# Two transformer blocks on one core: the order at the norms, at the start, in the logits, and the mixing of two attention maps

## The reference

```python
for i in range(4):                                   # first block
    q, k, v, ..., qm = split_cols(x @ w_in_...)
    mix = dsa_attention / dilated_attention / moba_attention(q, k, v, ...)
    mo  = memory_attention(qm, *split(layer_norm(mem) @ w_mem_kv[i]))
    x = layer_norm(ALPHA * x + concat(mix, mo) @ w_out[i], ln1_g[i], ln1_b[i])
    x = layer_norm(ALPHA * x + (silu(g) * u) @ w_down[i], ln2_g[i], ln2_b[i])   # g, u = x @ w_gate_up[i]
for l in range(2):                                   # second block
    h = rms_norm(x, norm_pre[l]);  u = h @ w_in[l]
    # differential attention: two softmax maps of each of four heads
    s  = einsum('bqhmd,bkhmd->bhmqk', q, k) * scale + bias
    pm = softmax(s)
    oa = einsum('bhqk,bkhe->bqhe', pm[:, :, 0] - lam * pm[:, :, 1], v)
    oa = rms_norm(oa, da_subln[l]) * (1 - lam_init)
    ...                                              # latent and sliding-window attention, three gated branches
    x = x + rms_norm(y @ w_out[l], norm_post[l])
    x = x + sigmoid(x @ w_ple_gate[l]) * (p[l] @ w_ple_proj[l])
```

## Time and profile before

| what | value |
|---|---|
| median of 3 runs | 1969.3 us (1964.08 to 1973.55) |
| profiled execution, its own time | 1971.21 us |
| its span, first to last instruction | 1969.2 us |
| mean granted clock of PE | 0.988 |
| PE busy | 1892.0 us, 9682 matmul records |
| DVE, ACT, POOL busy | 817.6, 938.9, 1520.2 us |

### The profile page before, as it was taken

The page is one execution under the profiler, slowest core; times in us unless marked ns, Lnnn a source line. Parts: engine busy times, 40 slices in busy tenths (PEclk is TensorE's granted clock), DMA queues, the critical chain, the costliest instruction groups (busy, mean ns, idle before and its releaser), DMA issues.

```text
span 1969.2 us, 27526 instructions
## 1 busy us (share of the span) xinstructions
PE 1892.0 (96%) x9682; PEld 1551.4 (79%) x9682; DVE 817.6 (42%) x1921; ACT 938.9 (48%) x1473; POOL 1520.2 (77%) x1332
## 2 busy tenths in 40 slices
PE   7999999999999999999999999989899999989998
PEld 6777888777888887788887688877888877878876
DVE  7774111356211345411067621035736344545634
ACT  4454444354444346444335644444447644545752
POOL 7767979885797987697977778795677886777784
PEclk9999999999999999999999999999999999999999
DMA  8444656564666564466545456654544555554452
GB/s 280 121 145 148 194 152 233 172 183 134 181 191 211 156 192 150 147 185 198 189 144 162 159 154 178 211 184 117 165 149 146 172 170 179 156 169 137 136 172 93
DMA packets 184269, 330.54 MB, mean 168 GB/s; under 512 B 12188, under 2 KB 44488, under 8 KB 184136
## 3 DMA queue, kind: packets, MB, share of 16 engines
q1 hardware_dynamic: 176224, 323.21, 53.1%
q10 hardware_dynamic: 7912, 5.59, 1.0%
HBM read 325.35 MB, written 3.41 MB: 167 GB/s over the span
## 4 chain that ended last, share of the span: by engine, by line
PE 79%; DVE 8%; POOL 7%; DMA 3%; issue 2%; ACT 1%; ACTq 0%; DVEq 0%
PE acc L1376 22%; PE acc L1378 22%; PE acc L1377 21%; POOL w_lo L1160 7%; PE tps L1327 4%; PE acc L1391 3%; PE tps L1409 2%; PE ops L1433 2%; DMA raw<-in_w_down 1%; DVE U L1798 1%; DVE small L1485 1%; PE acc L1351 1%; PE acc L1352 1%; PE acc L1353 1%; PE ops L1339 1%
## 5 line engine op out<-in xcount | busy, mean ns | idle before, releaser
L1160 POOL TENSOR_TENSOR w_lo<-raw,w_hi 128x512 fp32r<-128x512 f32 (+2 forms) x1244 | 1479.5, 1226 | 411.5 <-ACT w_hi L1188 410.2
L1188 ACT CAST w_hi<-raw 128x1024 fp32r<-128x1024 f32 (+2 forms) x624 | 615.8, 991 | 765.7 <-PE acc L1378 641.1
L1376 PE MATMUL acc<-w_hi,xT_hi 128*128 128x512 f32 (+1 forms) x1808 | 696.5, 385 | 17.7 <-issue 6.9
L1378 PE MATMUL acc<-w_hi,xT_lo 128*128 128x512 f32 (+1 forms) x1808 | 675.5, 374 | 0.0
L1377 PE MATMUL acc<-w_lo,xT_hi 128*128 128x512 f32 (+1 forms) x1808 | 675.2, 373 | 0.0
L1376 PEld LDWEIGHTS acc<-w_hi,xT_hi 128*128 128x128 f32 x1808 | 343.3, 190 | 91.3 <-issue 30.8
L1378 PEld LDWEIGHTS acc<-w_hi,xT_lo 128*128 128x128 f32 x1808 | 342.6, 189 | 60.4
L1377 PEld LDWEIGHTS acc<-w_lo,xT_hi 128*128 128x128 f32 x1808 | 343.7, 190 | 52.3
L1688 DVE TENSOR_TENSOR H<-G,acc 128x512 f32<-128x512 f32 (+1 forms) x48 | 30.9, 644 | 338.7 <-PE acc L1378 338.7
L1376 PE MATMUL acc<-w_hi,hT_hi 128*128 128x512 f32 x352 | 139.1, 395 | 4.6 <-POOL w_lo L1160 4.6
L1378 PE MATMUL acc<-w_hi,hT_lo 128*128 128x512 f32 x352 | 137.3, 390 | 0.0
(11 more groups left out here) (192 smaller groups left out, 1972.6 us busy)
## 6 DMA issues: line engine op xcount, KB each, us to landing
raw<-in_w_gate_up SPq DMA_DIRECT2D x160, 512.0 KB, 3.8
raw<-in_w_in SPq DMA_DIRECT2D x104, 512.0 KB, 3.7
raw<-in_w_down SPq DMA_DIRECT2D x88, 512.0 KB, 3.7
raw<-in_w_out SPq DMA_DIRECT2D x48, 512.0 KB, 3.5
raw<-in_w_in_a SPq DMA_DIRECT2D x32, 512.0 KB, 4.6
raw<-in_w_in_b SPq DMA_DIRECT2D x20, 512.0 KB, 3.8
raw<-in_w_mem_kv SPq DMA_DIRECT2D x16, 512.0 KB, 4.4
raw<-in_w_gate_up SPq DMA_DIRECT2D x32, 256.0 KB, 2.8
```

The costliest lines, as they stand in the source:

```text
L1160: ins = nc.gpsimd.tensor_tensor(w_lo[:, r, i, 0:ch.width], raw[:, r, i, 0:ch.width], w_hi[:, slot, i, 0:ch.width].bitcast(F32), ALU.subtract)
L1188: nc.scalar.copy(w_hi[:, u.u % SPLIT, 0:u.nk, 0:u.chunk.width], raw[:, u.u % RAW, 0:u.nk, 0:u.chunk.width]).then_inc(S["hi_ready"], 1)
L1376: nc.tensor.matmul(o, hi[:, tok], wh, start=first_k, stop=False)
L1378: ins = nc.tensor.matmul(o, lo[:, tok], wh, start=False, stop=last_k)
```

## The change

Six edits:

- `closing`: for the second chunk of `w_out`, of `w_down`, of `w_out_2` and of `w_ple_gate_2` the last two units of half 0 follow unit n - 7 and n - 6 of half 1 as counted from that chunk's end, in place of n - 5. The chunks of one weight are now made by two calls.
- A product unit on turned tiles waits for the high parts, multiplies them by both weight parts for both k tiles, then waits for the low parts and multiplies those. In the plan such units follow the high part's copy.
- Differential attention: a new DVE task `mix_maps` adds the second map, times -lam and the ratio of the two sums, to the first, in place in SBUF; one turn in place of two; six value records in place of twelve; the output scales one result. `combine` multiplies by the first map's sum as well.
- `do_scores` loops over halves outside and maps inside.
- Unit 0 is loaded between the two halves of `x`, units 1 to 9 ahead of `mem`, the gains and the constants.
- One semaphore more, `maps_mixed`.

```diff
-        self.turns = 1 if flavour == "dilated" else len(q)
+        self.turns = 1 if flavour in ("dilated", "differential") else len(q)
...
-                               [self.units[n - RAW].mm[1]] if n >= RAW else [], prio=1 if n >= 4 else -1, lat=2000)
+                               [self.units[n - RAW].mm[1]] if n >= RAW else [], prio=1 if n >= RAW else -3 if n == 0 else -1, lat=2000)
...
-                after = [u.low, *u.fed[t]]
+                after = [u.low, *[k.it.hi if k.kind == "take" and not flip else k for k in u.fed[t]]]
...
                     if n < self.normed + SPLIT:
                         last = min(last, self.normed - 1)
+                    if closing and k0 >= k_tiles - 2 * UK:
+                        last = len(self.units) - 1 - (k0 - (k_tiles - UK)) // UK - LAG - 2 + 1
                     after += [self.units[last].mm[1]] if last >= 0 else []
...
                 done = s.probs
-                if s.flipped:
+                if s.flavour == "differential":
+                    done = s.mixed = self.task("DVE", "mix_maps", s, 700, "maps_mixed", [s.combine], prio=0)
+                elif s.flipped:
...
-        x_in.append(p.task("SP", "x", t, 1500, f"x_landed{t}", prio=-1, lat=2500, inc=16))
+        x_in.append(p.task("SP", "x", t, 1500, f"x_landed{t}", prio=2 * t - 4, lat=2500, inc=16))
...
-                      v=[(da, 1024 + P * i)] * 2, out=P * i, dv=P, flavour="differential", mask="bias",
+                      v=[(da, 1024 + P * i)], out=P * i, dv=P, flavour="differential", mask="bias",
...
-                for f in u.fed[t][-1:]:
-                    pe.wait_ge(S[f.sem], max(g.n for g in u.fed[t]))
+                turned = [f for f in u.fed[t] if f.kind == "take" and not ch.flip]
+                if turned:
+                    pe.wait_ge(S["t_hi"], max(f.it.hi.n for f in turned))
...
-                    nc.tensor.matmul(o, hi[:, tok], wl, start=False, stop=False)
-                    ins = nc.tensor.matmul(o, lo[:, tok], wh, start=False, stop=last_k)
+                    ins = nc.tensor.matmul(o, hi[:, tok], wl, start=False, stop=False)
+                    if not turned:
+                        ins = nc.tensor.matmul(o, lo[:, tok], wh, start=False, stop=last_k)
+                if turned:
+                    pe.wait_ge(S["t_taken"], max(f.n for f in turned))
+                    for i in range(u.nk):
+                        ins = nc.tensor.matmul(acc[:, bank, 0:ch.width], act_tile(ch.acts, u.k0 + i)[1][:, P * t:P * t + P],
+                                               w_hi[:, u.u % SPLIT, i, 0:ch.width], start=False,
+                                               stop=u.k0 + i == ch.k_tiles - 1)
...
-                for m in range(s.maps):
-                    (qt, base, n), (kt, kbase, _) = s.q[m], s.k[m]
-                    for t in range(T):
-                        c = tile_cols(s, t)
+                for t in range(T):
+                    c = tile_cols(s, t)
+                    for m in range(s.maps):
+                        (qt, base, n), (kt, kbase, _) = s.q[m], s.k[m]
...
-                if not s.flipped:
-                    pe.wait_ge(S["probs_ready"], s.probs.n)
+                if s.flavour == "differential":
+                    pe.wait_ge(S["maps_mixed"], s.mixed.n)
...
-                    ins = v.tensor_scalar(rc[:, 2:4], rc[:, 2:4], neg_lam[:, s.layer:s.layer + 1], None, ALU.mult)
+                    ins = v.scalar_tensor_tensor(out=rc[:, 2:4], in0=rc[:, 2:4], scalar=neg_lam[:, s.layer:s.layer + 1],
+                                                 in1=sm[:, 0:2], op0=ALU.mult, op1=ALU.mult)
...
-            def combined_heads(s):
+            def heads_out(s):
...
                 for t in range(T):
-                    ins = v.scalar_tensor_tensor(out=to[:, t, :], in0=o[:, 0, t], scalar=rc[:, t:t + 1], in1=to[:, t, :],
-                                                 op0=ALU.mult, op1=ALU.add)
+                    ins = v.tensor_scalar(to[:, t], o[:, t], recips[:, s.slot, t:t + 1], None, ALU.mult)
...
+            def mix_maps(s):
+
+                lg, rc = step_logits(s), recips[:, s.slot, :]
+                dve.wait_ge(S["combined"], s.combine.n)
+                for t in range(T):
+                    c = tile_cols(s, t)
+                    ins = v.scalar_tensor_tensor(out=lg[:, 0, c], in0=lg[:, 1, c], scalar=rc[:, 2 + t:3 + t], in1=lg[:, 0, c],
+                                                 op0=ALU.mult, op1=ALU.add)
+                ins.then_inc(S["maps_mixed"], 1)
```

More of the change, by code:

```diff
@@ L225, in __init__ @@
         self.combine = None
+        self.mixed = None
         self.normal = [None, None]
@@ L428, in open_chunk @@
     def open_chunk(self, weight, k_tiles, acts, spec, fed=((), ()), clear=((), ()), banks=None, hold=((), ()),
-                   rows=None, flip=False):
+                   rows=None, closing=False, flip=False):
         col, width, how, dst = spec
@@ L532, in attention @@
             elif s.flavour == "differential":
-                s.outputs = self.task("DVE", "outputs", s, 2100, "out_taken", [s.values, s.combine], prio=0)
+                s.outputs = self.task("DVE", "outputs", s, 1700, "out_taken", [s.values], prio=0)
             s.values.release = s.outputs
@@ L750, in plan @@
             out = lin(w["w_out"][l], 8, "mixed", spec[:1], banks=[[(0,)], [(1,)]], rows=MIXED)
-        out += lin(w["w_out"][l], 8, "mixed", spec[1:], hold=[[scored]] * T, banks=ANY, rows=MIXED)
+        out += lin(w["w_out"][l], 8, "mixed", spec[1:], hold=[[scored]] * T, banks=ANY, rows=MIXED, closing=True)
         norm_tiles("layer_norm", g, [[ch.take[t] for ch in out] for t in range(T)], "x", out)
@@ L768, in plan @@
         g = p.gain("ln2_g", "ln2_b", l, up.units[-1].load)
-        down = lin(w["w_down"][l], FF // P, "h", [(c, n, "residual", c) for c, n in column_chunks(0, D)])
+        spec = [(c, n, "residual", c) for c, n in column_chunks(0, D)]
+        down = lin(w["w_down"][l], FF // P, "h", spec[:1])
+        down += lin(w["w_down"][l], FF // P, "h", spec[1:], closing=True)
         u_clear = [down[-1].units[-1].mm[1]]
@@ L891, in plan @@
         g = p.gain("norm_post_2", None, l)
-        out = lin(w["w_out_2"][l], 8, "x", [(c, n, "stats", c) for c, n in column_chunks(0, D)])
+        spec = [(c, n, "stats", c) for c, n in column_chunks(0, D)]
+        out = lin(w["w_out_2"][l], 8, "x", spec[:1])
+        out += lin(w["w_out_2"][l], 8, "x", spec[1:], closing=True)
         proj = lin(w["w_ple_proj_2"][l], 2, "s", [(c, n, "copy", (ple_out, c)) for c, n in column_chunks(0, D)])
         norm_tiles("rms_post", g, [[ch.take[t] for ch in out] for t in range(T)], "x", out, apply=1500)
-        pg = lin(w["w_ple_gate_2"][l], 8, "x", [(c, n, "sigmoid", ("bank",)) for c, n in column_chunks(0, D)])
+        spec = [(c, n, "sigmoid", ("bank",)) for c, n in column_chunks(0, D)]
+        pg = lin(w["w_ple_gate_2"][l], 8, "x", spec[:1])
+        pg += lin(w["w_ple_gate_2"][l], 8, "x", spec[1:], closing=True)
         last = l == DEPTH_2 - 1
@@ L1361, in products @@
                     pe.wait_ge(S[h.sem], h.n)
-                for f in u.fed[t][-1:]:
-                    pe.wait_ge(S[f.sem], max(g.n for g in u.fed[t]))
+                turned = [f for f in u.fed[t] if f.kind == "take" and not ch.flip]
+                if turned:
+                    pe.wait_ge(S["t_hi"], max(f.it.hi.n for f in turned))
+                else:
+                    for f in u.fed[t][-1:]:
+                        pe.wait_ge(S[f.sem], max(g.n for g in u.fed[t]))
                 if t == 0:
@@ L1916, in take_turn @@
                               tps[:, s.turn[j].slot[0], 0:blocks * P]).then_inc(S["t_taken"], 1)
[L1918 to L1920 removed]
+            def heads_out(s):
                 dve.wait_ge(S["pv_ready"], s.values.n)
[L1922 to L1923 removed]
+                o = ops[:, s.values.slot[0], 0:T * P].rearrange("p (t e) -> p t e", t=T)
+                spread = small[:, 6, 0:6 * T].rearrange("p (t c) -> p t c", t=T)
                 to = rows(s.heads_out)[:, :, s.out:s.out + P]
                 for t in range(T):
[L1926 to L1930 removed]
+                    ins = v.tensor_scalar(to[:, t], o[:, t], recips[:, s.slot, t:t + 1], None, ALU.mult)
                 ins.then_inc(S["out_taken"], 1)
                 dve.wait_ge(S["out_taken"], s.outputs.n)
[L1933 removed]
                 for t in range(T):
[L1935 removed]
+                    ins = v.bn_stats(spread[:, t, :], to[:, t])
                 link(ins)
@@ L1951, in outputs @@
                     return
-                combined_heads(s)
+                heads_out(s)
             def gate_output(s):
@@ L1976, in _ @@
                     combine(k.it)
+                elif k.kind == "mix_maps":
+                    mix_maps(k.it)
                 elif k.kind == "gate_output":
```

2 lines of the change are left out of this document (1 added, 1 removed).

## The result

The changed kernel takes 1954.7 us in the median of 16 runs, the kernel before 1969.1 us in 16 of its own on the same chips; the ratio is 0.9933, with a 95% interval of 0.9921 to 0.9945. By the ratio that is 13 us faster (the medians lie 14 apart), where 32 were predicted.

The account below looks back on a forecast made before the run. PE, busy 96% of the span, was taken to bound the kernel. Terms 22 + 2 + 9 + 0 - 1 = 32 us gave 1971.2 - 32 - 1.9 = 1937 us; forecast 1927 to 1947 (0.55), range 1915 to 1964.

Parts of the forecast that it names:

- What bounds the kernel: PE, busy 96% of the span and carrying 79% of the chain; only its records and gaps can move the time.
- The lead at the norms: At the norms half 0 ends 7 units before half 1 in place of 5, closing PE's gaps: 22 us won.
- the 3.4 us that the sum has for it: Half clock on PE behind two `w_out` norms: 1.7 us regained at each, counted in the lead's 22 us.
- the lead is not taken: Rival: PE's written order need not bring the lead; only the low copy's 5.4 us remains at eight norms; 1954 us, chance 0.16.
- The split wait: PE awaits the low part later, saving a 0.67 us copy: 5.4 us at eight norms within the lead, 2 us elsewhere.
- The mix: Differential attention's maps mixed by DVE: PE saves 1.02 us at each of eight steps; 9 us won with the gate's gap.
- the 2.4 us: Cost of one mix on DVE by the shared-port rule alone, with POOL at work 77% of the span; 1.8 was taken.
- the rival named for it: The mix takes the place of what it saves: PE waits up to 23 us over eight steps; 1948 to 1960, chance 0.13.
- The logits: Two maps' logits issued next to each other on PE: they already ran at once, so 0 us; rival 1919 us, 0.06.
- The start: Weights loaded ahead of memory: at most 3.4 us won at the first product, DVE's table slowed; 1 us lost taken.
- The upper end: Of the start's range of -3 to +11: eleven DVE table operations lengthen by 1 us each if POOL stays at work.
- POOL's stock: Slower rival: the lead empties POOL's low parts, PE stands 5.1 us at each of 8 norms; 2001 us, chance 0.06.

Follow-up runs that it names:

- e_first: The whole change plus half 1's last units of a closing chunk placed ahead of half 0's next-stage units; 1934.2 us, 0.9833 of the kernel before.

## Why the prediction was half right

**What bounds the kernel**: right. PE is busy 96% before and after, and what was won or lost in time was gaps and clock.

**The lead at the norms, 22 us**: this is the step that failed. Lead and split wait together gave 7.7 us (5 to 11) of the 24 reckoned for them. The sentence that fell is that "up to eight units of half 0 may run before it, 10.9 us, more than the chain". The units may, but the written order put four of them ahead of half 1's last unit, so they did not cover half 1's chain, they made it late. I had read the order of before at the norms after `w_out` and `w_down`, in which nothing of half 0 was free that early, and did not ask what else the plan would place once it was. Two smaller errors: at the two later `w_out` norms the lead has nothing to add (0.82 us stands); and for the `w_out_2` norms, costed at 0.3 us each because "the same products stand ahead of it", I did not see that in the kernel before four units of half 0 stood ahead of half 1's last unit too. They had 5.1 us to give at the first and, read in the same way, 3.9 at the second.

With that one priority turned round the kernel without the mix is 36 us faster than the kernel before, of which the start has 5. That the 31 us left come near the 24 reckoned is partly luck. Some 9 of them come from the two `w_out_2` norms, reckoned at 0.6. And the clock behind the gaps counts for far more than the 3.4 us that the sum has for it: 16 us between the two profiled executions, while the change itself gave next to nothing of it back (0.990 before and after). It is luck, too, that the measured 1954.7 us lies at the 1954 of the rival "the lead is not taken": the lead is taken, since half 0's turn at 677.08 waits for nothing.

**The split wait**: right, and a little more than reckoned: 10 us alone (6.5 to 13.2) against 5.4 and 2. The sum had no clock for it, but the mean granted clock rose from 0.990 to 0.993 in the median execution, some 6 us by the same estimate.

**The mix, 9 us**: wrong in size, 0 (within 2.4 us). PE's work fell by 8.6 us as reckoned, and a mix took 0.7 to 2.9 us a step, 1.6 in the mean where 1.8 was taken. POOL was at work in half of the mixes, not in 77%, so the 2.4 us were not reached. What failed is "I charge PE nothing of it" and "the gap itself loses only 0.6 us". PE's turn stands a guessed 0.7 us behind `combine`, so PE waits 4.2 us for the map; these waits make the gate's chain late again, while PE comes to the gate's turn earlier by its own savings: in the first layer that gap grows from 4.12 to 6.06 us, and over both layers it is 8.3 where it was 8.2. That is the rival named for it, at 9 of its 23 us. Not every microsecond of the 8.6 has been placed.

**The logits, 0**: right, with the number that the earlier trace rows gave.

**The start, 1 us lost**: wrong, 4 us won (1.8 to 6.7; 5 in e_first). DVE's table ended 1.4 us later, not 11: ACT's sine stood at 24.34 in place of 22.91. With the early start alone the wait of 3.43 us has become two of 1.33 and 1.39, PE waits for the memory's norm (`QT`) 1.8 us where it was 1.7, and a wait of 2.13 us behind it is gone. That accounts for part of the 4 us; where the rest lies is open. The upper end was real too, by another way than reckoned: one operation, 9.61 us, in one of two profiled executions.

**POOL's stock**, the slower rival: it did not come, 8.1 us of waits in 19.

So of 32 us, 24 + 9 - 1, the runs have 7.7 + 0 + 4.3, which is 12, and 13 measured.

## What to carry to other kernels

Where the order of work is written by a planner, a relaxed dependency does not only let the wanted work go early: ask which other task becomes free by it, and which of two free tasks the priority takes. A unit that another engine's long chain hangs on must go ahead of work that is only there to fill. And work taken off the bounding engine is worth nothing, as the mix was, while the chain that it waits for next has not become shorter by as much.

## What the runs showed of the hardware

One DVE operation with two inputs in SBUF (128x512, beside POOL's operations of the same kind) lasted 1.06 us in one execution and 9.61 us in another of the same kernel. In the first POOL and DVE took turns; in the second the record of the DVE operation begins at 34.52 and ends at 44.13, 0.56 us after POOL's run of twelve low parts, 28.72 to 43.57, was over. The Trainium skill, "SBUF — State Buffer", section "SBUF: two separate sides", says that whichever of the two starts first holds the shared ports for the whole instruction. The trace agrees in that DVE waited; and it shows that DVE can lose several times in a row, since about seven operations of POOL, 1.3 us each, began within the 9.61 us. How often that happens is left open: it was seen in one of the profiled executions with the early start, of which there were seven.

The mix shows the two prices side by side: the same pair of operations took 0.74 us where POOL had nothing under way and up to 2.86 us beside its low parts.

Of the 42 us between the profiled executions of the kernel before and of e_first without the mix, 16 are PE's same 9682 records in less time, at a mean granted clock of 0.999 in place of 0.988; 26 are idle time.

Two maps on 64 rows each ran at once in either order of issue: 0.86 us for eight records, which start in pairs.
